# Retention gate by seven block products, head-norm squares on ScalarE, up-projection ordered by token half

## The reference, cut to what matters

```python
u = rmsnorm(h, norm_mix[l]); proj = u @ w_in[l]
q, k, v, g_ret, p, gates = jnp.split(proj, split_points, axis=-1)   # 1024 wide each, gates 2048
q = rotary(q.reshape(b, s, 4, 256)); k = rotary(k.reshape(b, s, 4, 256)) * (256 ** -0.5)
ret = retention(q, k, v.reshape(b, s, 4, 256))                      # decayed scores, then values
ret = ret * lax.rsqrt(jnp.mean(ret * ret, axis=-1, keepdims=True) + NORM_EPS)   # per head
ret = ret.reshape(b, s, 1024) * jax.nn.silu(g_ret)
pool_out = multiscale_pool(p, pool_w[l], pool_scale[l])
gate = jax.nn.sigmoid(gates.reshape(b, s, 2, 1024) + gate_bias[l])
merged = gate[:, :, 0] * (ret @ w_ret_up[l]) + gate[:, :, 1] * (pool_out @ w_pool_up[l])
h = h + merged @ w_out[l]
```

## Time and profile before

| | |
|---|---|
| median of 3 runs | 1188.58 us (1188.36 to 1188.71) |
| profiled execution: time | 1188.89 us |
| its span, first to last instruction | 1187.2 us |
| TensorE matmul busy | 1177.9 us (99%), 5704 matmuls |
| VectorE busy | 951.2 us (80%) |
| ScalarE busy | 690.2 us (58%) |
| GpSimd busy | 168.3 us (14%) |
| granted TensorE clock | 0.999 |
| DMA | 221.96 MB, mean 187 GB/s |

### The profile page before, as it was taken

The page is one execution under the profiler, slowest core; times in us unless marked ns, Lnnn a source line. Parts: engine busy times, 40 slices in busy tenths (PEclk is TensorE's granted clock), DMA queues, the critical chain, the costliest instruction groups (busy, mean ns, idle before and its releaser), DMA issues.

```text
span 1187.2 us, 14701 instructions
## 1 busy us (share of the span) xinstructions
PE 1177.9 (99%) x5704; PEld 976.9 (82%) x5704; DVE 951.2 (80%) x1158; ACT 690.2 (58%) x827; POOL 168.3 (14%) x170
## 2 busy tenths in 40 slices
PE   9999999999999999999999999999999999999997
PEld 8777888888888888888888888888899888888886
DVE  7788798878778798878788887569997766988884
ACT  7775656656547666554565555657562445566642
POOL 2100132210200132120031220000000100222200
PEclk9999999999999999999999999999999999999999
DMA  9434565447343555555455555652784344555540
GB/s 342 173 132 159 185 246 182 177 177 272 132 142 104 216 198 189 184 210 200 155 193 196 214 213 171 253 210 86 245 306 172 136 159 175 197 200 182 188 173 36
DMA packets 32872, 221.96 MB, mean 187 GB/s; under 512 B 3777, under 2 KB 4289, under 8 KB 7074
## 3 DMA queue, kind: packets, MB, share of 16 engines
q1 hardware_dynamic: 32514, 219.77, 51.4%
q0 software_dynamic: 144, 1.05, 0.5%
q10 hardware_dynamic: 144, 0.20, 0.0%
HBM read 219.95 MB, written 1.05 MB: 186 GB/s over the span
## 4 chain that ended last, share of the span: by engine, by line
PE 98%; issue 1%; DVE 1%; DMA 0%; ACT 0%; SPq 0%; POOLq 0%; POOL 0%; DVEq 0%; ACTq 0%
PE ps L305 30%; PE ps L307 30%; PE ps L306 30%; PE ps L310 5%; PE ps L313 3%; DMA raw<-in_w 0%; ACT whi L257 0%; DVE h L472 0%; DVE AR L2829 0%; DVE st L1878 0%; SPq L2851 0%; DVE AR L1896 0%; DVE AR L2477 0%; ACT whi L274 0%; ACT AR L2820 0%
## 5 line engine op out<-in xcount | busy, mean ns | idle before, releaser
L264 DVE SCALAR_TENSOR_TENSOR wlo<-raw,whi 128x2048 fp32r<-128x2048 f32 x164 | 375.2, 2295 | 75.7 <-ACT whi L257 48.4
L257 ACT CAST whi<-raw 128x2048 fp32r<-128x2048 f32 x166 | 317.7, 1916 | 172.0 <-PE ps L307 164.0
L305 PE MATMUL ps<-whi,xh 128*128 128x512 f32 x1000 | 394.3, 394 | 0.0
L307 PE MATMUL ps<-whi,xl 128*128 128x512 f32 x1000 | 389.8, 390 | 0.0
L306 PE MATMUL ps<-wlo,xh 128*128 128x512 f32 x1000 | 389.7, 390 | 0.0
L305 PEld LDWEIGHTS ps<-whi,xh 128*128 128x128 f32 x1000 | 187.7, 188 | 44.6 <-issue 1.6
L307 PEld LDWEIGHTS ps<-whi,xl 128*128 128x128 f32 x1000 | 187.7, 188 | 40.1
L306 PEld LDWEIGHTS ps<-wlo,xh 128*128 128x128 f32 x1000 | 187.9, 188 | 36.9
L305 PE MATMUL ps<-whi,yh 128*128 128x512 f32 x344 | 138.2, 402 | 0.0
L307 PE MATMUL ps<-whi,yl 128*128 128x512 f32 x344 | 134.4, 391 | 0.0
L306 PE MATMUL ps<-wlo,yh 128*128 128x512 f32 x344 | 134.0, 390 | 0.0
(11 more groups left out here) (293 smaller groups left out, 1447.8 us busy)
## 6 DMA issues: line engine op xcount, KB each, us to landing
raw<-in_w SPq DMA_DIRECT2D x198, 1024.0 KB, 4.8
raw<-in_w SPq DMA_DIRECT2D x4, 512.0 KB, 7.6
h<-in_x SPq DMA_DIRECT2D x4, 256.0 KB, 5.2
raw<-in_w SPq DMA_DIRECT2D x4, 256.0 KB, 4.6
AR<-in_b_pw SPq DMA_DIRECT2D x1, 1024.0 KB, 4.9
AR<-in_gate_bias SPq DMA_DIRECT2D x1, 1024.0 KB, 6.9
raw<-in_w POOLq DMA_DIRECT2D x1, 1024.0 KB, 8.2
AR<-in_dft SPq DMA_DIRECT2D x1, 864.0 KB, 7.5
```

What stands on the lines that cost most here:

```text
L257: e.copy(whi[:, v % S, :], raw_at(v)).then_inc(*sig.up("hi", v))
L264: e.scalar_tensor_tensor(out=wlo[:, v % S, :], in0=raw_at(v), scalar=1.0, in1=whi[:, v % S, :].bitcast(F32), op0=ALU.mult, op1=ALU.subtrac ...
L305: e.matmul(o, ah, bh, start=start, stop=False, skip_group_check=skip)
L307: return e.matmul(o, al, bh, start=False, stop=stop, skip_group_check=skip)
```

## The change

1. `UNITS`, `RET`, `GROUPS`: g_ret becomes a group `gr` of seven units; 4 raw units give 7 (the stage has 50 in place of 47). All four sums are made on VectorE (for g0, one is an adding DMA). The first sum has a place of its own per group.
2. `gr` uses banks 4, 5, 6 and collects in the place of the rotated queries and keys, so `scalar_part` waits for the last scores. Silu works in place in SBUF.
3. The squares and sums of the head norm: eight ScalarE `Square` activations of 256 columns with accumulation. VectorE adds the epsilon. The scale by the root and the gate are one instruction per head and token tile.
4. The up-projection takes first token tile 0 of ru0 and ru1, then tile 1; ru uses banks 0, 1, 4, 5. The orders of the engines are rewritten for this, and the Silu table is loaded by an explicit instruction after the last sigmoid.

```diff
-       "q1": 2, "k1": 2, "gr0": 2, "gr1": 2, "ru0": 2, "ru1": 2, "out": 4}
-GROUPS = ("v", "g0")
+       "q1": 2, "k1": 2, "gr": 7, "ru0": 2, "ru1": 2, "out": 4}
+GROUPS = ("v", "g0", "gr")
-        first_sum = ar(7680, UC)
+        first_sum = {RU["v"]: ar(7680, UC), RU["g0"]: ar(7680, UC), RU["gr"]: ar(0, UC)}
-        KIND = {"v": vn}
-        GBANK = {"v": (4, 5, 6), "g0": (2, 3, 0), "g1": (4, 5, 2)}
+        KIND = {"v": vn, "gr": ar(7680, 2, 1024)}
+        GBANK = {"v": (4, 5, 6), "gr": (4, 5, 6), "g0": (2, 3, 0), "g1": (4, 5, 2)}
...
@@ scalar_part
-            q.wait_ge(*banks.filled("pooled", 3))
+            q.wait_ge(*(banks.filled("sc", 3) if g == "gr" else banks.filled("pooled", 3)))
@@ scalar_ret_norm, after the two copies of L2435
+            for t in range(2):
+                q.wait_ge(*banks.emptied("pv", t, j))
+                for n in range(2):
+                    c = 512 * j + 256 * n
+                    q.wait_ge(*sig.last("sumsq"))
+                    e.activation(ar(5120, 256), vn[:, t, c:c + 256], ACT.Square, bias=0.0, scale=1.0 / 16,
+                                 accum_out=ret_sums(j, t)[:, n:n + 1]).then_inc(*sig.up("sumsq", "ret", j, t, n))
@@ vector_ret_norm: L2447, L2450 and vector_ret_scale (L2459) go
+                q.wait_ge(*sig.at("sumsq", "ret", j, t, 1))
+                e.tensor_scalar(s2, s2, EPS, None, ALU.add).then_inc(*sig.up("ret_var", j, t))
@@ scalar_ret_gate
+            g = group_dst("gr", t, j)
+            q.wait_ge(*group_done("gr", j, t))
+            e.activation(g, g, ACT.Silu, bias=0.0, scale=1.0).then_inc(*sig.up("gate_sig", "gr", j, t))
@@ vector_ret_gate
+            for n in range(2):
+                v = vn[:, t, 512 * j + 256 * n:512 * j + 256 * n + 256]
+                d = e.scalar_tensor_tensor(out=v, in0=v, scalar=ret_sums(j, t)[:, n:n + 1], in1=g[:, 256 * n:256 * n + 256],
+                                           op0=ALU.mult, op1=ALU.mult)
@@ tensor_ret, the new order whole, from the end of k1
+            tensor_product(e, q, "gr", 0)
+            tensor_product(e, q, "gr", 1)
             tensor_ret_scores(e, q, 2)
             tensor_ret_scores(e, q, 3)
+            tensor_product(e, q, "gr", 2)
+            tensor_product(e, q, "gr", 3)
             tensor_ret_values(e, q, 2)
             tensor_ret_values(e, q, 3)
+            tensor_product(e, q, "gr", 4)
             turn_x(e, q, "ret", None, 0, 0, vn[:, 0, :], "y", sig.at("gated", 0, 0))
+            tensor_product(e, q, "gr", 5)
+            tensor_product(e, q, "gr", 6)
+            quarter(e, q, "ru0", RU["ru0"], 0, 0, 0, yh, yl, y_ret)
+            quarter(e, q, "ru1", RU["ru1"], 0, 0, 1, yh, yl, y_ret)
+            turn_x(e, q, "ret", None, 0, 1, vn[:, 0, :], "y", sig.at("gated", 1, 0))
+            quarter(e, q, "ru0", RU["ru0"], 0, 1, 0, yh, yl, y_ret)
             turn_x(e, q, "ret", None, 1, 0, vn[:, 1, :], "y", sig.at("gated", 0, 1))
+            quarter(e, q, "ru1", RU["ru1"], 0, 1, 1, yh, yl, y_ret)
             turn_x(e, q, "ret", None, 1, 1, vn[:, 1, :], "y", sig.at("gated", 1, 1))
+            quarter(e, q, "ru0", RU["ru0"], 1, 0, 4, yh, yl, y_ret)
+            quarter(e, q, "ru0", RU["ru0"], 1, 1, 4, yh, yl, y_ret)
             turn_x(e, q, "merge", None, 0, 0, merged[:, 0, :], "x", sig.at("merged", 0, 0))
+            quarter(e, q, "ru1", RU["ru1"], 1, 0, 5, yh, yl, y_ret)
             turn_x(e, q, "merge", None, 1, 0, merged[:, 1, :], "x", sig.at("merged", 0, 1))
+            quarter(e, q, "ru1", RU["ru1"], 1, 1, 5, yh, yl, y_ret)
@@ scalar_ret, from the norm of the second half (units gr + 7, + 8 are ru0, + 9, + 10 ru1)
+            hi(e, q, RU["ru0"])
             scalar_ret_norm(e, q, 1)
+            scalar_part(e, q, "gr", 2)
+            split_turned_act(e, q, "y", "ret", 0, 0, yh, None, sig.at("y_free", "pool"))
+            hi(e, q, RU["ru0"] + 1)
             scalar_ret_gate(e, q, 1, 0)
+            hi(e, q, RU["ru1"])
+            scalar_part(e, q, "gr", 3)
+            hi(e, q, RU["ru1"] + 1)
+            split_turned_act(e, q, "y", "ret", 0, 1, yh)
@@ vector_ret, the same stretch
+            lo(e, q, RU["gr"] + 6)
+            lo(e, q, RU["ru0"])
+            vector_part(e, q, "gr", 1)
+            split_turned_dve(e, q, "y", "ret", 0, 0, yh, yl)
+            vector_ret_norm(e, q, 1)
+            lo(e, q, RU["ru0"] + 1)
+            lo(e, q, RU["ru1"])
+            vector_ret_gate(e, q, 1, 0)
+            vector_part(e, q, "gr", 2)
+            vector_part(e, q, "gr", 3)
+            split_turned_dve(e, q, "y", "ret", 0, 1, yh, yl)
+            lo(e, q, RU["ru1"] + 1)
+            vector_ret_gate(e, q, 0, 1)
```

More of the change, by code:

```diff
@@ L231, in raw_at @@
         def raw_at(v):
-            return first_sum if raw_of[v] is None else raw[:, raw_of[v] % R, :]
+            return first_sum[v - 1] if raw_of[v] is None else raw[:, raw_of[v] % R, :]
         def raw_loaded(v):
@@ L2466, in scalar_ret_gate @@
         def scalar_ret_gate(e, q, j, t):
[L2467 to L2471, removed]
-        def vector_ret_gate(e, q, j, t):
[L2474 to L2477, removed]
+            g = group_dst("gr", t, j)
+            q.wait_ge(*group_done("gr", j, t))
+            e.activation(g, g, ACT.Silu, bias=0.0, scale=1.0).then_inc(*sig.up("gate_sig", "gr", j, t))
+        def vector_ret_gate(e, q, j, t):
+            g = group_dst("gr", t, j)
+            q.wait_ge(*sig.at("gate_sig", "gr", j, t))
+            q.wait_ge(*sig.at("ret_rstd", j, t))
+            for n in range(2):
+                v = vn[:, t, 512 * j + 256 * n:512 * j + 256 * n + 256]
+                d = e.scalar_tensor_tensor(out=v, in0=v, scalar=ret_sums(j, t)[:, n:n + 1], in1=g[:, 256 * n:256 * n + 256],
+                                           op0=ALU.mult, op1=ALU.mult)
+            d.then_inc(*sig.up("gated", j, t))
         def tensor_ret(e, q):
@@ L2552, in tensor_ret @@
[L2552 to L2556, removed]
+            tensor_product(e, q, "gr", 5)
+            tensor_product(e, q, "gr", 6)
+            sig.alias("x_free", ("nm",), "made", ("gr", 6))
+            quarter(e, q, "ru0", RU["ru0"], 0, 0, 0, yh, yl, y_ret)
@@ L2564, in tensor_ret @@
-            quarter(e, q, "ru1", RU["ru1"], 1, 1, 1, yh, yl, y_ret)
+            quarter(e, q, "ru1", RU["ru1"], 1, 0, 5, yh, yl, y_ret)
             turn_x(e, q, "merge", None, 1, 0, merged[:, 1, :], "x", sig.at("merged", 0, 1))
-            sig.alias("y_free", ("ret",), "full1", ("ru1", 1))
+            quarter(e, q, "ru1", RU["ru1"], 1, 1, 5, yh, yl, y_ret)
+            sig.alias("y_free", ("ret",), "full5", ("ru1", 1))
             u = RU["out"]
@@ L2643, in scalar_ret @@
             hi(e, q, RU["k1"] + 5)
+            hi(e, q, RU["gr"] + 4)
+            scalar_part(e, q, "gr", 0)
+            scalar_part(e, q, "gr", 1)
+            hi(e, q, RU["gr"] + 5)
+            hi(e, q, RU["gr"] + 6)
             scalar_ret_gate(e, q, 0, 0)
-            hi(e, q, RU["gr0"] + 4)
-            scalar_ret_gate(e, q, 0, 1)
+            hi(e, q, RU["ru0"])
             scalar_ret_norm(e, q, 1)
-            hi(e, q, RU["gr0"] + 5)
+            scalar_part(e, q, "gr", 2)
+            split_turned_act(e, q, "y", "ret", 0, 0, yh, None, sig.at("y_free", "pool"))
+            hi(e, q, RU["ru0"] + 1)
             scalar_ret_gate(e, q, 1, 0)
-            split_turned_act(e, q, "y", "ret", 0, 0, yh, None, sig.at("y_free", "pool"))
+            hi(e, q, RU["ru1"])
+            scalar_part(e, q, "gr", 3)
+            hi(e, q, RU["ru1"] + 1)
+            split_turned_act(e, q, "y", "ret", 0, 1, yh)
+            for j in range(2):
+                scalar_ret_gate(e, q, j, 1)
             split_turned_act(e, q, "y", "ret", 1, 0, yh)
[L2652 to L2655, removed]
             split_turned_act(e, q, "y", "ret", 1, 1, yh)
             hi(e, q, RU["ru0"] + 4)
+            split_turned_act(e, q, "x", "merge", 0, 0, xh, None, sig.at("x_free", "nm"))
             hi(e, q, RU["ru0"] + 5)
-            split_turned_act(e, q, "x", "merge", 0, 0, xh, None, sig.at("x_free", "nm"))
+            split_turned_act(e, q, "x", "merge", 1, 0, xh)
             hi(e, q, RU["ru1"] + 4)
-            split_turned_act(e, q, "x", "merge", 1, 0, xh)
             hi(e, q, RU["ru1"] + 5)
@@ L2739, in vector_ret @@
                     lo(e, q, RU[key] + 4 + t)
+            vector_group_sum(e, q, "gr", 1)
+            vector_group_sum(e, q, "gr", 6)
             vector_ret_scores(e, q, 0)
@@ L2745, in vector_ret @@
             lo(e, q, RU["q1"] + 5)
+            vector_group_sum(e, q, "gr", 4)
             vector_ret_norm(e, q, 0)
[L2747 to L2753, removed]
+            vector_rotary(e, q, "k1", 0)
+            lo(e, q, RU["gr"] + 2)
+            vector_rotary(e, q, "k1", 1)
@@ L2754, in vector_ret @@
+            lo(e, q, RU["gr"] + 3)
+            vector_group_sum(e, q, "gr", 5)
             vector_ret_scores(e, q, 2)
             vector_ret_scores(e, q, 3)
-            vector_ret_gate(e, q, 0, 1)
```

(13 more changed lines are left out.)

27 lines of the change are left out of this document (8 added, 19 removed).

## The result

The changed kernel takes 1190.93 us (median of 14 runs, 1190.15 to 1192.72), the kernel before 1188.86 us (14 runs, 1188.36 to 1189.32). The ratio is 1.0019, 95% interval [1.0012, 1.0026]: slower by 2.1 us, beside a forecast of 1190.8 and a range of 1188.1 to 1192.8. The runs of the changed kernel spread over 2.6 us, those of before over 1.0.

What follows compares the result with a forecast made beforehand. TensorE, 99% busy, was taken as the bound. Terms −2.77 + 0.2 + 2.95 + 1.75 + 0.25 gave +2.4 us, stepping through the order +2.2, which was taken: median 1190.8 us, range 1188.1 to 1192.8.

Steps and rivals of the forecast that it cites:

- signs named: 84 gr matmuls for 96; waits of 2.5 to 3 us before product 5, 1.5 to 1.7 before ru0 (0,1); full clock.
- The products: Seven block products replace eight in gr: 2.42 us gained on TensorE's path, together −2.77 with the old wait gone.
- old wait: TensorE's 0.5 us wait on a turned tile's low part in the kernel before; going, it saves some 0.35 us.
- Added work, priced at nothing: Net about +11 us on VectorE and about +12 us on ScalarE, fitting their slack: no cost on TensorE's path.
- Bank 5: Product 1 of gr waits for bank 5, freed by k1's second rotation: +0.2 us (0 to 0.4).
- Bank 6: Product 5 of gr shares bank 6 with the turn just ahead: stall 2.85 us, plus 0.1 for the restart.
- The turn of (0,1): Quarter ru0 (0,1) reads the tile turned directly ahead of it: stall 1.65 us (1.5 to 2.2), plus 0.1.
- The turn of (1,0): This turn needs a gated tile taking VectorE 3.05 us while quarter ru0 (0,1) takes 2.85: +0.25 us (0 to 0.7).
- The turn of merged: merged (0,1) ready about 975.3 for a turn at 975.4; 0 to 0.4 us could come.
- The clock: Rival, 6%: after the two stalls TensorE falls to 1.2 GHz for one or two products, 2.73 us each; 1193.5 to 1196.
- A: Rival, 8%: neither stall, before product 5 or ru0 (0,1), occurs; faster, 1185.8 to 1186.3 us.
- B: Rival, 11%: only the bank is not shared at product 5, the turn's stall stays; −0.5 us, 1188.1.

Runs made afterwards that it cites:

- e7: Both edits of e3, plus bank 7 for 5 in gr and the gated tile (1,0) made before ru1's low part; 1186.09 us, ratio 0.9977.
- e6: Kernel before with one part of the change alone: head-norm squares and sums by eight ScalarE activations; 1188.73 us, ratio 0.9999.
- e5: Changed kernel with ScalarE's four squares of the second head norm moved behind the copy of turned tile (0,0); 1190.15 us, ratio 1.0011.
- e2: Changed kernel with the turn of (0,1) one quarter earlier, before ru1 (0,0); bank 6 stays shared; 1190.35 us, ratio 1.0008.
- e8: Kernel of e2 with eight extra matmuls filling the wait before product 5; 1188.61 us, ratio 0.9999.
- e4: Changed kernel with eight extra matmuls of 512 columns, result unread, in the wait before product 5; 1190.71 us, ratio 1.0018.
- e1: Changed kernel with product 5 of gr collecting in PSUM bank 2 in place of bank 6; 1188.49 us, ratio 0.9997.
- e3: Changed kernel with bank 2 for product 5 and the turn of (0,1) one quarter earlier; 1186.75 us, ratio 0.9983.

## Why the prediction was right

The steps of the sum, in its order, with what the trace of after has. Of the signs named, both waits came, the first at 2.4 us where 2.5 to 3 was named, and no new wait of over 1 us for another engine appeared elsewhere; the clock was not full throughout.

- **The products.** Forecast −2.77 with the old wait. With one wait of 0.2 us left the stretch is 54.76 against 57.51 (e7): −2.75.
- **Added work, priced at nothing.** Forecast +11 us on VectorE and +12 on ScalarE, none on the path; measured +10.7 and +11.4, and e7, which carries all of it, keeps the gain. The squares alone are free in the kernel before (e6); in the changed one they stand in the chain of the bank-6 term, where moving them gives back 0.43 us (e5).
- **Bank 5.** Forecast 0.2; product 1 starts 0.33 us after the matmul ahead in place of 0.23, and the next 0.34 behind: 0.2.
- **Bank 6.** Forecast a stall of 2.85; measured 946.17 − 943.77 = 2.40. The place and the chain were right, one size was off: four squares and reads took 2.09 us from 941.97 to 944.06, 0.52 each, where I took 0.64. A square of 256 columns took 0.418 us, as the slope of the earlier trace rows gave (0.42); too much was what I added for a square to wait for the one before. The Trainium skill's budget (*ScalarE: Activation LUTs*, "Rules for kernel authors") would give 0.51 for the square, an estimate, and is further off.
- **The turn of (0,1).** Forecast 1.65; measured 960.90 − 958.89 − 0.36 = 1.65.
- **The turn of (1,0).** Forecast 0.25; 960.90 to 963.98 is 3.08 where a restarted quarter takes 2.85: 0.23. The turn of merged was on time.

These steps add up to +1.73, and the stretch without the clock has +1.80, against +2.2 in the forecast. The 0.1 that I added to each stall for the restart was hardly there: behind a stall the second matmul starts 0.33 us after the first, behind an unstalled turn 0.32. Nine of the fourteen runs lie between 1190.15 and 1191.04, that is 1188.86 + 1.3 to + 2.2.

- **The clock (D, 6%).** This rival came in part, beside the forecast and not in its place: of the fourteen runs, five are at 1191.77 and more, with a granted clock of 0.997 or 0.998 (others show 0.998 to 1.000). Only the profiled one of them shows the fall itself. I had priced it at 2.73 us for each product; it was 1.59, since the fall ended within product 5. It moves the median little. The rival's first sentence rests on a misreading: the wait of 1.4 us in the earlier trace rows is the one before the kernel's first matmul, at 1.36 us, so the trace of before shows no clock held over such a wait; between two matmuls of it no more than 0.9 us pass from start to start. That the clock can stay full behind such a wait is shown only by the traces of the change, as by after before ru0 (0,1). That the median met the forecast within 0.2 us is partly luck: the squares gave 0.4 to 0.5 less, and such runs pull up.
- **A and B** fell: the turn does have bank 6, and a quarter does wait for a tile turned just ahead of it.

By the prediction's bound of 0.2% the result stands on the line, 1.0019 with an interval that reaches to both sides of it, as the chances 0.48 and 0.46 had it.

## What to carry to other kernels

When TensorE is 99% busy, a rewrite that takes products away pays only if each new edge in its order has cover: list every PSUM bank that a new product shares with the step just ahead of it, and put at least one product between a turned tile and its first reader (the round trip here is 2.0 us, a product 2.73). A wait of two microseconds on an otherwise dense TensorE may cost more than itself; if it can't be removed, useless matmuls in it may be worth their place (the median fell by 1.7 us from e2 to e8, but by only 0.2 from after to e4). Price an instruction chain by the distances of starts, and the summed load of the helping engines only where their queue stands ahead of the critical one.

## What the runs showed of the hardware that I had not expected

In the profiled execution of after TensorE ran at its full level, 2.4 GHz, from 7.5 us on, with no more than 0.9 us between the starts of two matmuls, until it stood 2.16 us. Matmuls of 512 columns then followed at 0.43 us in place of 0.23, at a granted clock of 0.50, the 1.2 GHz level, for 3.41 us. With the same wait in e2 the profiled execution keeps its clock and its time is that of the lower group; seven runs lie 1.2 to 2.3 us above that group. With waits of 1.73 and 1.41 us (e5) the profiled execution has no fall and the runs no second group. With the wait filled there is none either (e8, on the other chip than e2). That the standing is a cause is thus well supported, though the fall itself was recorded once; what decides between executions is open. The slow stretch coincides with a full DMA load (1.01 of 16 engines, 425 GB/s), but e2's profiled execution has the same load, 1.00 and 0.96, and no fall.

Single runs about 2 us over their group (e1 at 1190.52, e3 at 1188.62, e4 at 1192.65 and 1192.81) may be another matter. The profiled one of e4 lost its time in the kernel's first 14 us, where its matmuls of 512 columns still took 0.42 us from start to start at 9.4 us and those of after 0.24 at 7.5; whether the others did is not shown.
